# Residual rows and final-norm weight loaded into the expert weights' ring slots, and an unrolled combination

## What is computed

```
hn  = rms_norm(h, norm2_w)
y_e = (silu(hn @ w_gate[e]) * (hn @ w_up[e])) @ w_down[e]     for the rows sent to expert e
h   = h + gate_0 * y_e0 + gate_1 * y_e1                       the two chosen experts of each row
out = h * rsqrt(mean(h*h) + 1e-6) * final_norm_w
```

## Time and profile before

| what | us |
|---|---|
| median of three runs | 2356.72 |
| lowest and highest | 2350.95, 2357.32 |
| the profiled execution | 2356.02 |
| its span, from first to last instruction | 2354.3 |
| busy in the span: TensorE | 1992.0 |
| VectorE | 1197.4 |
| ScalarE (ACT) | 802.8 |
| GpSimd (POOL) | 374.5 |

### The profile page before, as it was taken

The page is one execution under the profiler, slowest core; times in us unless marked ns, Lnnn a source line. Parts: engine busy times, 40 slices in busy tenths (PEclk is TensorE's granted clock), DMA queues, the critical chain, the costliest instruction groups (busy, mean ns, idle before and its releaser), DMA issues. The chain is left out here.

```text
span 2354.3 us, 29680 instructions
## 1 busy us (share of the span) xinstructions
PE 1992.0 (85%) x11958; PEld 1787.7 (76%) x11958; DVE 1197.4 (51%) x1226; ACT 802.8 (34%) x1145; POOL 374.5 (16%) x372
## 2 busy tenths in 40 slices
PE   7999999899959998878767399895699999999950
PEld 7999999888859998767644399874578888888840
DVE  5334433156541210343353455423678888888836
ACT  4211111034312210212221121212367777777722
POOL 0000000254421001110112100000621111111004
PEclk9999999899968886989878699897799999999975
DMA  6345554544364642432321753434889999999937
GB/s 213 117 155 159 175 187 141 176 138 122 98 167 123 168 123 78 126 103 78 92 82 35 251 181 89 166 115 160 274 333 403 400 409 406 408 400 404 404 116 263
DMA packets 209467, 473.00 MB, mean 201 GB/s; under 512 B 34599, under 2 KB 166087, under 8 KB 196274
## 3 DMA queue, kind: packets, MB, share of 16 engines
q1 hardware_dynamic: 139842, 318.45, 38.6%
q0 software_dynamic: 16688, 73.60, 9.2%
q10 hardware_dynamic: 52800, 79.05, 9.2%
HBM read 376.12 MB, written 121.93 MB: 212 GB/s over the span
## 5 line engine op out<-in xcount | busy, mean ns | idle before, releaser
L2719 DVE TENSOR_TENSOR k_w_lo<-expert_raw,k_w_hi 128x4096 fp32r<-128x4096 f32 x96 | 424.2, 4420 | 78.6 <-ACT k_w_hi L2663 78.4
L2663 ACT CAST k_w_hi<-expert_raw 128x4096 fp32r<-128x4096 f32 x96 | 348.5, 3632 | 107.1 <-PE k_pu L74 67.9
L72 PE MATMUL a_acc<-a_w_hi,x_hi 128*128 128x256 f32 x648 | 186.5, 288 | 0.2 <-DVE x_lo L229 0.2
L74 PE MATMUL a_acc<-a_w_hi,x_lo 128*128 128x256 f32 x648 | 184.5, 285 | 0.0
L73 PE MATMUL a_acc<-a_w_lo,x_hi 128*128 128x256 f32 x648 | 184.5, 285 | 0.0
L72 PEld LDWEIGHTS a_acc<-a_w_hi,x_hi 128*128 128x128 f32 x648 | 125.7, 194 | 0.7 <-DVE x_lo L229 0.5
L73 PEld LDWEIGHTS a_acc<-a_w_lo,x_hi 128*128 128x128 f32 x648 | 125.7, 194 | 0.0
L74 PEld LDWEIGHTS a_acc<-a_w_hi,x_lo 128*128 128x128 f32 x648 | 125.5, 194 | 0.0
L572 PE MATMUL e_gate_acc<-x_hi,e_gate_w_hi 128*128 128x384 f32 (+1 forms) x192 | 77.9, 406 | 52.0 <-DVE e_gate_w_lo L558 52.0
L948 PE MATMUL d_z_acc<-d_z_w_hi,x_hi 128*128 128x256 f32 x288 | 99.4, 345 | 16.4 <-DVE d_z_w_lo L934 14.7
L72 PE MATMUL k_po<-k_w_hi,k_h_hi 128*128 128x512 f32 x256 | 102.5, 400 | 10.6 <-DVE k_h_lo L2740 10.6
(11 more groups left out here) (445 smaller groups left out, 5067.7 us busy)
## 6 DMA issues: line engine op xcount, KB each, us to landing
expert_raw<-in_w_expert_gate SPq DMA_DIRECT2D x32, 2048.0 KB, 10.2
expert_raw<-in_w_expert_up SPq DMA_DIRECT2D x32, 2048.0 KB, 12.0
expert_raw<-in_w_expert_down SPq DMA_DIRECT2D x32, 2048.0 KB, 11.5
scratch_o_moe<-k_out ACTq DMA_DIRECT2D x32, 512.0 KB, 11.4
a_w<-in_w_in SPq DMA_DIRECT2D x15, 1024.0 KB, 7.1
scratch_u_tm<-h ACTq DMA_DIRECT2D x81, 128.0 KB, 2.0
scratch_o_moe<-h_zeros POOLq DMA_DIRECT2D x2, 4096.0 KB, 19.4
out_s_kv<-in_cache_kv_w POOLq DMA_DIRECT2D x8, 1008.0 KB, 8.3
```

The source lines that it names most:

```text
L72: nc.tensor.matmul(out, one_pass(a_hi), one_pass(b_hi), start=(i == 0), stop=False)
L74: last = nc.tensor.matmul(out, one_pass(a_lo), one_pass(b_hi), start=False, stop=(i == n - 1))
L2663: nc.scalar.copy(one_pass(w_hi[:, kind, :]), raw[:, c % NRAW, :]).then_inc(s_hi, 1)
L2719: nc.vector.tensor_tensor(one_pass(w_lo[:, kind, :]), raw[:, c % NRAW, :], w_hi[:, kind, :], ALU.subtract).then_inc(s_lo, 1)
```

## The change

The residual rows and the final norm's weight are loaded by SP in the experts' phase, behind the last weight, into ring slots whose last weight has been split: tiles 0 to 3, tiles 4 to 7, tile 8, then the weight, on `s_lo` of 93, 94, 95. SP waits for them at the end of that phase. `expert_raw` lives on to the end, and `h_rows` and its load are gone. In the combination the loop is written out, the gathers take their lists from `slots` directly, and `idx`, its copy, the semaphores `s_free`, `s_idx` and `s_seen` and the load of the weight are gone; POOL waits on `s_sum` instead of `s_free`.

```diff
+ROWS_IN_SLOT = WEIGHT // D
+def last_rows(T, t, m):
+    slot = (3 * NE - NRAW + t // ROWS_IN_SLOT) % NRAW
+    return T["expert_raw"][:, slot, :].rearrange("p (t c) -> p t c", c=D)[:, t % ROWS_IN_SLOT:t % ROWS_IN_SLOT + m, :]
...
                     sp.dma_start(raw[:, c % NRAW, :], expert_weight(T, c)).then_inc(s_raw[c % NRAW], 16)
+                for t in range(0, TILES, ROWS_IN_SLOT):
+                    m = min(ROWS_IN_SLOT, TILES - t)
+                    sp.wait_ge(s_lo, 3 * NE - NRAW + t // ROWS_IN_SLOT + 1)
+                    sp.dma_start(last_rows(T, t, m), T["h"][t * 128:(t + m) * 128, :].rearrange("(t p) c -> p t c", p=128)
+                                 ).then_inc(s_last, 16)
+                sp.dma_start(last_rows(T, TILES, 1)[:, 0, :], T["final_norm_w"].broadcast_to([128, D])).then_inc(s_last, 16)
+                sp.wait_ge(s_last, 16 * (1 + -(-TILES // ROWS_IN_SLOT)))
...
-                for half in range(2):
-                    sp.dma_start(T["h_rows"][:, :, half * D // 2:(half + 1) * D // 2],
-                                 T["h"].rearrange("(t p) c -> p t c", p=128)[:, :, half * D // 2:(half + 1) * D // 2]
-                                 ).then_inc(s_h, 16)
                 blocks(sp, body)
-                sp.wait_ge(s_h, 32)
...
-            @block.sync
-            def _(sp):
-                sp.dma_start(w[:, :], T["final_norm_w"].broadcast_to([128, D])).then_inc(s_w, 16)
-                with pool.Fori(0, 3) as j:
-                    for u in range(3):
-                        pool.wait_ge(s_free, j * 3 + (u + 1))
-                        nc.gpsimd.tensor_copy(idx[:, u, :], T["slots"][:, ds(j * 3 + u, 1), :].rearrange("p a k -> p (a k)")
-                                              ).then_inc(s_idx, 1)
-                        pool.wait_ge(s_idx, j * 3 + (u + 1))
-                        pool.sem_inc(s_seen, 1)
-                        for k in range(2):
-                            pool.indirect_dma_start(out=o[:, u, k, :], out_offset=None, in_=T["o_moe"],
-                                                    in_offset=bass.IndirectOffsetOnAxis(ap=idx[:, u, k:k + 1], axis=0)
-                                                    ).then_inc(s_o[u], 16)
+                for n in range(TILES):
+                    u = n % 3
+                    if n >= 3:
+                        pool.wait_ge(s_sum, n - 2)
+                    for k in range(2):
+                        pool.indirect_dma_start(out=o[:, u, k, :], out_offset=None, in_=T["o_moe"],
+                                                in_offset=bass.IndirectOffsetOnAxis(ap=T["slots"][:, n, k:k + 1], axis=0)
+                                                ).then_inc(s_o[u], 16)
...
                     dve.sem_inc(s_sum, 1)
-                    dve.sem_inc(s_free, 1)
...
         with living(("expert_raw", [128, NRAW, WEIGHT])):
-            run(phase_experts)
-        with living(("h_rows", [128, TILES, D])):
-            run(phase_overflow, phase_combine)
+            run(phase_experts, phase_overflow, phase_combine)
```

More of the change, by code:

```diff
@@ L2580, in across @@
             return bc(ap.unsqueeze(1), [128, TILES, n])
-        s_const = sm("const")
+        s_const, s_last = sm("const"), sm("last")
         s_raw = [sm(f"raw{i}") for i in range(NRAW)]
@@ L2980, in phase_overflow @@
         s_seen = sm("seen")
-        s_h = sm("h")
         s_tab, s_id, s_row, s_w, s_xt, s_xe, s_gu, s_silu, s_hid, s_ht, s_hte, s_down, s_out, s_done = (
@@ L3089, in sm @@
             return sem(f"m_{name}")
-        w, eps, junk, ms = sb("w", [128, D]), sb("eps", [128, 1]), sb("junk", [128, D]), sb("ms", [128, 3, 2])
-        h = T["h_rows"]
+        w, eps, junk, ms = last_rows(T, TILES, 1)[:, 0, :], sb("eps", [128, 1]), sb("junk", [128, D]), sb("ms", [128, 3, 2])
+        h = [last_rows(T, n, 1)[:, 0, :] for n in range(TILES)]
         o, y = sb("o", [128, 3, 2, D]), sb("y", [128, 3, D])
-        idx = sb("idx", [128, 3, 2], i32)
-        s_seen = sm("seen")
-        s_w, s_eps, s_idx = sm("w"), sm("eps"), sm("idx")
+        s_eps = sm("eps")
         s_o, s_st = ([sm(f"{n}{u}") for u in range(3)] for n in ("o", "st"))
-        s_free, s_sum, s_rms, s_y = sm("free"), sm("sum"), sm("rms"), sm("y")
+        s_sum, s_rms, s_y = sm("sum"), sm("rms"), sm("y")
         with nc.Block() as block:
-            @block.sync
-            def _(sp):
-                sp.dma_start(w[:, :], T["final_norm_w"].broadcast_to([128, D])).then_inc(s_w, 16)
             @block.gpsimd
             def _(pool):
-                with pool.Fori(0, 3) as j:
-                    for u in range(3):
-                        pool.wait_ge(s_free, j * 3 + (u + 1))
-                        nc.gpsimd.tensor_copy(idx[:, u, :], T["slots"][:, ds(j * 3 + u, 1), :].rearrange("p a k -> p (a k)")
-                                              ).then_inc(s_idx, 1)
-                        pool.wait_ge(s_idx, j * 3 + (u + 1))
-                        pool.sem_inc(s_seen, 1)
-                        for k in range(2):
-                            pool.indirect_dma_start(out=o[:, u, k, :], out_offset=None, in_=T["o_moe"],
-                                                    in_offset=bass.IndirectOffsetOnAxis(ap=idx[:, u, k:k + 1], axis=0)
-                                                    ).then_inc(s_o[u], 16)
+                for n in range(TILES):
[6 more added lines that the diff above has]
+                                                ).then_inc(s_o[u], 16)
             @block.vector
@@ L3121, in _ @@
                 nc.vector.memset(eps[:, :], EPS).then_inc(s_eps, 1)
-                dve.sem_inc(s_free, 3)
-                dve.wait_ge(s_w, 16)
                 def summed(n):
@@ L3128, in summed @@
                     for k in range(2):
-                        nc.vector.scalar_tensor_tensor(h[:, n, :], o[:, u, k, :], T["gates"][:, n, k:k + 1], h[:, n, :],
-                                                       ALU.mult, ALU.add)
+                        nc.vector.scalar_tensor_tensor(h[n], o[:, u, k, :], T["gates"][:, n, k:k + 1], h[n], ALU.mult, ALU.add)
                         dve.drain()
                     dve.sem_inc(s_sum, 1)
-                    dve.sem_inc(s_free, 1)
                 def normalised(n):
@@ L3141, in normalised @@
                         dve.wait_ge(s_st[u], n // 3 * 16)
-                    nc.vector.scalar_tensor_tensor(y[:, u, :], h[:, n, :], ms[:, u, 1:2], w[:, :], ALU.mult, ALU.mult)
+                    nc.vector.scalar_tensor_tensor(y[:, u, :], h[n], ms[:, u, 1:2], w, ALU.mult, ALU.mult)
                     dve.drain()
@@ L3157, in squares @@
                     act.wait_ge(s_sum, n + 1)
-                    nc.scalar.activation(junk[:, :], h[:, n, :], ACT.Square, accum_out=ms[:, u, 0:1])
+                    nc.scalar.activation(junk[:, :], h[n], ACT.Square, accum_out=ms[:, u, 0:1])
                     act.drain()
```

## The result

The changed kernel took 2329.63 us in the median of four runs (2326.49 to 2334.08), the kernel before 2356.34 in four (2350.95 to 2357.32): ratio 0.9893, 95% interval 0.9869 to 0.9917, **faster by about 1.1%**. The forecast was 2341.0 with a range from 2335 to 2348: the direction was right and the time too high by 11.4 us.

The account below looks back on a forecast made before the run. Bounds, in the tail: SP's 13.7 us wait for residual rows in the overflow block, then VectorE in the combination. Terms 13.3 + 0.6 + 0.4 + 0.5 + 0.6 = 15.4 us gave 2341.0, range 2335 to 2348.

Parts of the forecast that it names:

- The residual load leaves the overflow block: Overflow block: with SP's wait gone the barrier closes on TensorE, saving 13.3 us (10.7 to 13.7).
- The same load in the experts' phase: End of the experts' phase: loads in place by about 2260, over 18 us before the last store's issue; cost none.
- The rival of the moved wait: End of experts: SP stands there instead; landing 10 us late leaves a gain of 5.4, time 2351; chance 0.06.
- The cover was worth something: Rival, start of combination: instruction fetch without the long wait costs 2.6, combination gives nothing; gain 10.7 us, 2346; chance 0.17.
- The combination: Combination's terms: first gather 0.6, weight load 0.4, gather waits 0.5, VectorE's semaphore 0.6 us.
- First gather sooner: Start of combination: POOL's copy and waits go, so the first gather starts 0.6 us sooner (0 to 1.3).
- Weight load: Start of combination: the weight's load no longer holds back the first gathers, 0.4 us (0 to 1.7).
- Waits for gathers: Combination: without POOL's copy VectorE's later waits for gathers go, tile 1's stays; 0.5 us (0 to 1.1).
- a semaphore a tile: Combination: VectorE loses one semaphore instruction a tile, nine times 0.1, taken as 0.6 us (0 to 0.9).
- The gathers take their list badly: Rival, POOL in the combination: gathers with lists in `slots` take 4.16 us each, making it slower, 2370; chance 0.04.
- how the numbers follow: Whole time: chances of the cases, and the forecast's 2338 to 2346 widened by 3 and 2 from three runs' spread.

Follow-up runs that it names:

- h_early_only: Changed kernel's early residual loads with the old combination (loop, index copies, weight load): ratio 0.9943 to the kernel before; overflow 4.30 us, combination 54.24.
- wait_kept: Changed kernel, loading the residual rows a second time in the overflow block and waiting for them: ratio 0.9970 to the kernel before, overflow 17.10 us.
- unrolled_only: Kernel before with the new written-out combination, residual rows and weight loaded where they were: ratio 0.9989; overflow 17.67 us, combination 51.88.
- weight_late: Changed kernel with the final norm weight loaded at the start of the combination again: combination 51.15 us, first sum 7.04 behind the barrier.
- vector_event: Changed kernel with VectorE's second event a tile back: ratio 0.9941 to the kernel before, period 4.51 us, combination 53.29.
- copies_kept: Changed kernel with POOL's index copies back, written out without the loop: combination 51.24 us, first gather 0.81 behind the barrier.
- after_again: The changed kernel, unchanged, run again beside the kernel before: ratio 0.9913, runs from 2317.0 to 2343.0 us.
- pool_event: Changed kernel with an event that POOL counts up itself ahead of each pair of gathers back: ratio 0.9926 to the kernel before, combination 51.25 us.

## Why the prediction was right in direction and wrong in time

**The residual load leaves the overflow block: right.** 13.3 predicted, 13.39 measured, 13.4 in h_early_only, and given back by wait_kept. TensorE is the last to arrive, and its branch ends 0.8 us ahead of the second barrier's end.

**The same load in the experts' phase: right.** In place 21 us before the last store, the phase unchanged. The rival of the moved wait falls. The rate that the prediction worked with was a little off, without weight at such a slack: before, the two loads took 16.0 us from the first issue (2283.34) to the last landing (2299.31), not some 15, which is 0.30 MB a us in place of 0.31.

**The cover was worth something: not so.** Behind TensorE's branch (0.40 us, as before) no engine stands, and the first gather starts 0.77 behind the barrier. The 16 KB packet that had moved under the wait still moves, now at 2278.95, 0.7 us behind that branch (DMA from 2278.5 to 2280):

```profile
q8 instruction: 1, 0.02, 3.9%
```

In *unrolled_only* and *wait_kept* it moves under the wait, as before, and the first gather starts 0.77 behind the barrier there too: the cover was worth nothing to it. The Trainium skill's rule on taken branches (Runtime: NRT & Kernel Launch, Instruction fetch mechanics) would have let one expect a stall here; the trace shows none, though the packet comes without cover.

**The combination: 2.1 predicted, 3.0 measured**, in parts:
- First gather sooner, 0.6: it is 0.63 (1.40 to 0.77 behind the barrier). What counts is the landing of tile 1's pair, whose issue moved by 1.36 (4.62 to 3.26): the sum of tile 1 starts 0.98 sooner (11.25 to 10.27).
- Weight load, 0.4: nothing in weight_late, while unrolled_only leaves room for some tenths. It and the term above came to 1.0 together, right only as a sum.
- Waits for gathers, 0.5, and a semaphore a tile, 0.6: from the sum of tile 1 to the last multiplication 36.90 us became 35.57, 1.32 less, of which vector_event shows 0.77 for the event; 0.55 are left for the waits. I had put them down to the copy; with the copy back and no loop (copies_kept) they stay away, so they go with the loop, or with copy and event together.
- Not in the sum: the last multiplication starts 5.93 us before the end in before, 5.23 now, 0.70 less: 0.55 because the last store is done sooner (3.17 to 2.62, with no instruction packet beside it), and 0.15 in what follows it. The prediction had no term for either.

These are one execution of each. In the mean of three and of six, the same three stretches are 0.74, 1.74 and 0.71 shorter, 3.2 in all.

**The gathers take their list badly: not so.** They took 0.94 in the profiled execution, at worst 1.92 in another (after_again), and VectorE did not wait for them behind tile 1.

**The step that failed is in how the numbers follow.** I took three runs of before, 2350.95 to 2357.32, for the spread of a measurement and widened the range by 3 and 2. One kernel's runs lie 30 us apart: 137 of before reach from 2331.7 to 2364.1, median 2353.3, and 52 of the changed kernel from 2315.6 to 2343.0, median 2332.1. So the 11.4 us are: 3.4 by the base (2356.72 against 2353.3), 2.4 by the first four runs of the changed kernel (2329.63 against 2332.1), and 5.6 by the gain (21.3 between these medians against 15.7). Of the 5.6, 0.8 is the tail (16.5), about 0.7 more appears at equal clock (17.2), which is within two standard errors, 2.8 go with the clock, and 1.3 are medians against means (21.3 against 20.0). The profile held the warning: a sample attention at 0.80 in the mean of the two levels is a stretch whose length hangs on the clock, and nothing in the prediction priced that.

## What to carry to other kernels

A wait at a block's end that only holds a barrier was worth its distance to the next engine's arrival, here to 0.1 us, since the load's new place had slack. In a loop bound by one engine, price an edit by that engine's period and by the landing that starts it: here an earlier first sum bought nothing, and one event less a tile bought 0.1 us each time. Where a stretch runs at a clock between its two levels, no few runs show the spread: compare phase by phase, and let the range hold the clock.

## What was not expected of the hardware

- **The granted clock of one program differs from execution to execution**: 236.5 to 257.6 us for the same 1660 matmuls, and 30 us over the runs of a kernel.
- **A gather that starts while one of VectorE's 1.28 us instructions is at work ends 0.81 to 0.84 us behind that instruction's end.** It holds for all 142 such gathers of the profiled executions other than wait_kept. The first sum's first instruction in copies_kept ran from 2288.79 to 2290.07; the gather that began at 2288.91 ended at 2290.89. In after_again and pool_event it is the same: 10.38 + 1.28 + 0.81 = 12.47 and 10.79 + 1.28 + 0.81 = 12.88 us behind the barrier, ends of gathers that began at 10.55 and 11.08. One that starts just ahead of the instruction (17.63 against 17.69 in the changed kernel) takes 0.94. VectorE's instruction keeps its 1.28 in these cases; in wait_kept one took 1.32, with a gather that began 0.07 behind its start and kept its 0.94. The Trainium skill, SBUF — State Buffer, Who interferes with whom, has the two exclude each other: the trace agrees as to the gather. The prediction expected this by that page, without the size; here it costs VectorE nothing, since each pair has slack.
- **A gather followed a copy by 0.27 us when written out and by 0.81 to 0.85 in the loop.**
